# Moving transposes, norm sums, output gates and retention heads in the order of work of a one-core kernel of three blocks

## The reference

```python
# first block: normed and modulated x, projected to heads, joined by gates
o_g = gla_bidir(q, k, v, la_f, la_b, s0_f, s0_b)        # gated linear attention (GLA), 4 heads, values 128 wide
o_n = neighborhood_attention(q, k, v, k_ctx, v_ctx, rpb) # 8 heads of 64, the context as more keys
# each layer: x normed, then
#   MLA attention: keys and values from a normed low-rank part (kv), queries from a normed one (cq)
#   a convolution of 31 taps over the tokens, a norm over 512 channels, SiLU
#   retention: 4 heads of 256, attention weighted by a decay, a norm per head, a gate
# mix = sum over the branches of tanh_gate * (branch @ W), then out projection, norm, FFN, norm
```

## Time and profile before

| | us |
|---|---|
| median of 3 runs | 2898.34 |
| lowest, highest | 2896.63, 2902.26 |
| span of the profiled execution | 2895.1 |
| PE busy in it | 2824.8 |
| first block's attention stage, as PE's records show it | to about 534 |
| layer 0, layer 1 | about 902 to 1898, 1898 to 2893 |

### The profile page before, as it was taken

The page is one execution under the profiler, slowest core; times in us unless marked ns, Lnnn a source line. Parts: engine busy times, 40 slices in busy tenths (PEclk is TensorE's granted clock), DMA queues, the critical chain, the costliest instruction groups (busy, mean ns, idle before and its releaser), DMA issues.

```text
span 2895.1 us, 34427 instructions
## 1 busy us (share of the span) xinstructions
PE 2824.8 (98%) x13718; PEld 2245.6 (78%) x13718; DVE 1293.4 (45%) x1706; ACT 1133.0 (39%) x1687; POOL 1187.0 (41%) x539
## 2 busy tenths in 40 slices
PE   7999999999999999999999999999999999999999
PEld 6787678788888776787788888877767868788887
DVE  5776424511113866835315202277677353341123
ACT  4334643432233555433334222245545233442222
POOL 2123233354443662453444444435624434344442
PEclk9999999999999999999999999999999999999999
DMA  7343223332223211222232222222112212232222
GB/s 256 117 155 129 73 80 103 111 109 98 96 98 126 78 62 37 73 95 73 87 120 84 96 93 102 95 104 79 61 36 73 101 67 102 95 110 95 95 95 80
DMA packets 89278, 277.97 MB, mean 96 GB/s; under 512 B 9952, under 2 KB 10272, under 8 KB 89120
## 3 DMA queue, kind: packets, MB, share of 16 engines
q1 hardware_dynamic: 89120, 275.78, 27.1%
HBM read 268.40 MB, written 7.34 MB: 95 GB/s over the span
## 4 chain that ended last, share of the span: by engine, by line
PE 89%; DVE 8%; ACT 2%; issue 1%; DMA 0%; SPq 0%; DVEq 0%; ACTq 0%
PE bank L1680 23%; PE bank L1682 23%; PE bank L1681 23%; PE bank L1813 2%; PE bank L2006 2%; PE bank L1956 2%; PE bank L1706 1%; PE bank L1731 1%; PE bank L1729 1%; PE bank L1730 1%; PE bank L1698 1%; PE bank L1699 1%; PE bank L1968 1%; PE bank L1997 1%; DVE pageF L2815 1%
## 5 line engine op out<-in xcount | busy, mean ns | idle before, releaser
L2953 POOL TENSOR_TENSOR wlo<-wraw,whi 128x1024 fp32r<-128x1024 f32 x429 | 1040.9, 2429 | 1478.4 <-ACT whi L2035 1462.9
L1680 PE MATMUL bank<-pageR,whi 128*128 128x512 f32 x3184 | 1289.1, 405 | 6.4 <-ACT pageF L2288 1.6
L1682 PE MATMUL bank<-pageR,wlo 128*128 128x512 f32 x3184 | 1231.1, 387 | 0.0
L1681 PE MATMUL bank<-pageR,whi 128*128 128x512 f32 x3184 | 1229.9, 386 | 0.0
L1680 PEld LDWEIGHTS bank<-pageR,whi 128*128 128x128 f32 x3184 | 599.5, 188 | 161.9 <-issue 43.1
L1681 PEld LDWEIGHTS bank<-pageR,whi 128*128 128x128 f32 x3184 | 599.8, 188 | 135.9 <-issue 23.7
L1682 PEld LDWEIGHTS bank<-pageR,wlo 128*128 128x128 f32 x3184 | 598.7, 188 | 123.6
L2035 ACT ACTIVATE whi<-wraw 128x1024 fp32r<-128x1024 f32 x429 | 450.4, 1053 | 409.8 <-PE bank L1682 315.9
L2109 ACT ACTIVATE pageR<-pageF 128x512 fp32r<-128x512 f32 x136 | 85.9, 632 | 436.9 <-DVE pageF L2674 188.5
L2815 DVE SCALAR_TENSOR_TENSOR pageF<-pageF,prm 128x497 f32<-128x497 f32 (+9 forms) x180 | 200.1, 1112 | 2.7
L2669 DVE TENSOR_TENSOR pageF<-bank,pageF 128x512 f32<-128x512 f32 x44 | 30.4, 691 | 211.5 <-PE bank L1682 204.7
(11 more groups left out here) (236 smaller groups left out, 2618.3 us busy)
## 6 DMA issues: line engine op xcount, KB each, us to landing
wraw<-in_wst SPq DMA_DIRECT2D x429, 512.0 KB, 3.4
pageF<-in_wmod SPq DMA_DIRECT2D x96, 256.0 KB, 5.0
pageF<-in_xT SPq DMA_DIRECT2D x16, 256.0 KB, 4.1
pageF<-in_bias SPq DMA_DIRECT2D x16, 256.0 KB, 3.9
kept<-pageF SPq DMA_DIRECT2D x16, 256.0 KB, 4.9
pageF<-kept SPq DMA_DIRECT2D x16, 256.0 KB, 4.0
out_x<-pageF SPq DMA_DIRECT2D x8, 256.0 KB, 2.0
pageF<-in_cT SPq DMA_DIRECT2D x4, 256.0 KB, 10.0
```

The source lines that it names most:

```text
L1680: e.matmul(o, hi, xh, start=first, stop=False)
L1681: e.matmul(o, hi, xl, start=False, stop=False)
L1682: i = e.matmul(o, lo, xh, start=False, stop=last)
L2953: e.tensor_tensor(wlo[:, b % NH, :, :], wraw[:, b % NR, :, :], bc(whi[:, b % NH, :, :]), ALU.subtract).then_inc(*wlod.up(("wlo", b)))
```

## The change

It changes nothing of what is computed, only where steps stand in the plan. (1) Value transposes of GLA stand inside the projection that follows (`turn_gla`), behind its third yield, with heads 0 and 1 in one and 2 and 3 in another; those of the last neighbourhood pair go inside the first `w_ma` projection, and the empty yields beside them are gone. (2) The sums of the `cq`, convolution and retention norms stand one or two rounds later. (3) `side_ret` is a side of its own: it starts when the last pair of attention heads begins to write its values (`("half", l)`), takes its banks from `mb` and waits for pages. (4) `main_branch` runs up to 6 gates ahead, and while pages are short it waits and goes on when 8 are free.

```diff
--- before.py
+++ after.py
@@ -574,7 +574,7 @@
         yield
         for m in range(2):
             if m:
-                yield from proj("wk_g", m, H, HC)
+                yield from turn_gla(0, proj("wk_g", m, H, HC))
             rope_gla(("kg", m), ("o", "wk_g", m))
             if m:
                 evict(("kgc", m), ("oc", "wk_g", m), 256)
@@ -585,10 +585,13 @@
                     yield from proj("wv_g", h, H, HC)
                     evict(("vg_f", h), ("o", "wv_g", h))
                     evict(("vgc_f", h), ("oc", "wv_g", h), 256)
-                if h % 2:
-                    gla_values(h - 1)
+
+    def turn_gla(m, proj_next):
+        for i, _ in enumerate(proj_next):
+            if i == 2:
+                gla_values(2 * m)
+                gla_values(2 * m + 1)
             yield
-            gla_values(2 * m + 1)
 
     def gla_values(h):
         to_tokens(("vg", h), ("vg_f", h), ALL4, mb, ("vg_f", h))
@@ -746,9 +749,6 @@
             yield from proj("wq_na", m, H)
             evict(("raw", "qn", m), ("o", "wq_na", m))
             made.add(("raw", "qn", m))
-        yield
-        yield
-        na_values(3)
 
     def na_values(m):
         to_tokens(("vn", m), ("vn_f", m), ALL4, mb, ("vn_f", m))
@@ -847,7 +847,7 @@
         bias_load(0, 0)
         bias_load(1, 0)
         for h in range(4):
-            yield from proj("w_og", h, H)
+            yield from proj("w_og", h, H) if h else turn_gla(1, proj("w_og", h, H))
             pages.take(("og", h))
             step("silu_gate", h)
             mb.give(("o", "w_og", h), ("og", h))
@@ -883,7 +883,10 @@
     def main_gates1():
         for m in range(8):
             for nm in ("w_ma", "w_mb"):
-                yield from proj(nm, m, H)
+                for i, _ in enumerate(proj(nm, m, H)):
+                    if i == 2 and nm == "w_ma" and m == 0:
+                        na_values(3)
+                    yield
                 pages.take((nm, m))
                 step("tanh_gate", (nm, m), ("o", nm, m))
                 mb.give(("o", nm, m), (nm, m))
@@ -1098,7 +1101,7 @@
             s1.add(("kv", l), 0, ("kv", l))
             for m in range(2):
                 s2.add(("cq", l, m), 0, ("cq", l, m))
-            yield
+            yield from pause(2)
             r = yield from s1.rstd_steps(128, "ones", sbk)
             yield
             step("kv_normed", l)
@@ -1146,6 +1149,8 @@
                 if qt == 0:
                     sbk.take(("mlab", l, j))
                 step("mla_values", l, j, qt)
+                if j == 2 and qt == 0:
+                    made.add(("half", l))
                 for x in (h - 1, h):
                     pages.give(("pt", "mla", (l, x, qt)), ("av", "mla", l, j, qt))
                 if qt == 3:
@@ -1223,8 +1228,7 @@
             sq = Squares(p, ("conv", l))
             for m in range(4):
                 sq.add(("conv", l, m), 0, ("cc", l, m))
-            yield
-            yield
+            yield from pause(4)
             r = yield from sq.rstd_steps(512, "ones", sbk)
             yield
             for m in range(4):
@@ -1270,14 +1274,18 @@
                 pages.give(("tE", l, h, i), ("tD", l, h))
 
         def side_ret():
+            yield from p.ready(("half", l))
+            yield from p.room(8)
             ret_decay(0)
             for h in range(4):
                 yield from p.ready(("rg", l, h, 1))
+                yield from p.room(6)
                 for j in range(4):
-                    sbk.take(("rs", l, h, j))
+                    yield from p.free_banks(mb, 2)
+                    mb.take(("rs", l, h, j))
                     pages.take(("ra", l, h, j))
                     step("ret_scores", l, h, j)
-                    sbk.give(("rs", l, h, j), ("ra", l, h, j))
+                    mb.give(("rs", l, h, j), ("ra", l, h, j))
                     if j % 2:
                         yield
                 pages.give(("rq", l, h), ("rs", l, h, 3))
@@ -1285,18 +1293,18 @@
                 if h < 3:
                     ret_decay(h + 1)
                 for i in range(2):
-                    sbk.take(("ro", l, h, i))
+                    yield from p.free_banks(mb, 2)
+                    mb.take(("ro", l, h, i))
                     step("ret_values", l, h, i)
                     pages.give(("rv", l, h, i), ("ro", l, h, i))
-                    evict(("rof", l, h, i), ("ro", l, h, i), bks=sbk)
+                    evict(("rof", l, h, i), ("ro", l, h, i))
                     yield
                 for j in range(4):
                     pages.give(("ra", l, h, j), ("ro", l, h, 1))
                 sq = Squares(p, ("ret", l, h))
                 for i in range(2):
                     sq.add(("rof", l, h, i), 0, ("rof", l, h, i))
-                yield
-                yield
+                yield from pause(3)
                 r = yield from sq.rstd_steps(256, "ones", sbk)
                 yield
                 yield
@@ -1314,11 +1322,15 @@
             ahead = 0
             gate = lambda m: ("tg", l, 8 * i + m)
             xs = [(key, l, m) for m in range(n)]
-            while (not all(x in made for x in xs) or ahead < 3) and ahead < 4 and len(pages.free) >= 8:
-                yield from proj("w_gate" + L, 8 * i + ahead, X)
-                tanh_scaled(gate(ahead), ("o", "w_gate" + L, 8 * i + ahead))
-                ahead += 1
-            yield from p.ready(*xs)
+            while not all(x in made for x in xs) or ahead < 3:
+                if ahead < 6 and len(pages.free) >= 8:
+                    yield from proj("w_gate" + L, 8 * i + ahead, X)
+                    tanh_scaled(gate(ahead), ("o", "w_gate" + L, 8 * i + ahead))
+                    ahead += 1
+                elif all(x in made for x in xs):
+                    break
+                else:
+                    yield
             for m in range(8):
                 if m >= ahead:
                     yield from p.room(3)
@@ -1341,7 +1353,7 @@
         weave(chain(main_mla(), main_conv(0), main_conv(3), main_ret(0), main_conv(1), main_ret(1), main_conv(2),
                     main_branch(0, "o_mla", 4, "w_mo"), main_branch(1, "o_conv", 4, "w_pw"), main_ret(2), main_ret(3),
                     main_branch(2, "o_ret", 8, "w_ro")),
-              [chain(side_mla(), side_ret()), chain(taps(0), taps(1), taps(2)), taps(3), side_conv_norm()], 1)
+              [side_mla(), side_ret(), chain(taps(0), taps(1), taps(2)), taps(3), side_conv_norm()], 1)
         p.drop(X, ("o", "w_gate" + L, 23))
         pages.give(rs.r, ("tgs", ("tg", l, 23)))
         for name in ("cosr", "sinr"):
```

## The result

The changed kernel takes 2917.86 us (median of 4 runs, 2915.69 to 2919.93), the kernel before 2898.89 beside it: the ratio is 1.0067, with a 95% interval of 1.0053 to 1.0080, 19.0 us slower. I had forecast 2908.8 and a range up to 2917, so the sign was right and the size too small: 10 us were expected, 19 came, just beyond the range. The profiled span is 2916.9 against 2895.1. These 21.8 us are more than the 19.0 of the medians because the profiled execution of the kernel before was one of its quickest. In every run whose own time is listed beside its span, only about 2 us (1.8 to 2.05) lie around the span, not the 3.2 that I had taken.

A forecast was written before the change was run, and what follows sets the result against it. PE, busy 2824.8 of 2895.1 us, was taken as the bound. Two layers at -8.7, +1.6 once for the clock and +5.3 for the first block made 10.5 us slower: span 2905.6, median 2908.8, range 2885 to 2917.

The forecast's parts named there:

- part 5: Six gates ahead: empty rounds behind the convolution's sum leave a new 8.7 us wait before `w_pw`, -10.8 a layer.
- Rival A: Convolution's tail stays covered by at least five rounds of main work, so its loss becomes 0: 2887.2 us; chance 0.22.
- part 1: First block, moved GLA and last neighbourhood value transposes: a gain of 5.3 us (0 to 11).
- Gain 8.0 - 4.9 = 3.1: GLA values 0 and 1: 8.0 us lost before, 4.9 after with a new wait of 3.2 and lower clock.
- +0.5: GLA values 2 and 3 inside the first `w_og` projection: small gain in us (0 to 1.6), still lacking a bank.
- +5.3: Sum of all first-block terms, a gain in us (0 to 11).
- +2.7: First block, transposes at 249.54: their 2.68 us wait falls with the main work two rounds further on.
- part 2: Later norm sums: their waits, 4.8 us a layer, all go; net +4.5 a layer and +1.6 once for the clock.
- 1.4 a layer: Retention head 3: `o_ret` comes a round later, leaving one round less of cover before `w_ro`, a loss in us.
- parts 3 and 4: Retention beside the last attention heads: 8.8 us lost against 6.4 before, -2.4 a layer (+2 to -5).
- The 4.6: New wait in us of the retention head's value products for DVE's decays, standing 3.4 behind their first score.
- Rival C: Dearer: convolution's chain takes 12 us instead of 9, attention's end costs 3.5 a layer: 2917 us; chance 0.12.

The follow-up runs named there:

- cap8b1: The changed kernel with up to 8 gates ahead in branch 1 in place of 6: 2906.76 us, ratio 1.0029.
- gate_all: The kernel before with the new rule for gates ahead, and all 8 gates of branch 1 before its first product: 2892.01 us, ratio 0.9972.
- gate_only: The kernel before with the new rule for gates ahead alone (up to 6, going on when pages are free): 2911.62 us, ratio 1.0048.
- gla_only: The kernel before with the GLA value transposes moved, nothing else: 2902.59 us, ratio 1.0012.
- cq_only: The kernel before with one further round ahead of the kv and cq sums, nothing else: 2906.61 us, ratio 1.0025.
- cqsum: The kernel before with the cq sum alone one round later, the kv norm where it was: 2903.74 us, ratio 1.0017.
- sums_only: The kernel before with the convolution's sum two rounds and the retention heads' sums one round later, nothing else: 2898.98 us, ratio 1.0002.
- half_gate: The kernel before with retention as a side of its own from the half mark and the new rule for gates ahead: 2914.63 us, ratio 1.0051.
- gate_all_conv: The kernel before with the new gate rule, all 8 branch 1 gates before its first product, and the convolution's sum two rounds later: 2895.45 us, ratio 0.9987.

## Why the prediction was right and wrong, point by point

- **The tail of the convolution (part 5)**: right in place, mechanism and size. -10.8 was forecast; the wait of 8.1 and the slots behind it, 1.9 over their usual time, cost 10.0 in either layer. `cap8b1` and `gate_all` show it: cover put back behind the sum takes it away. Net of the sum's wait, the convolution was forecast at -6.8 in layer 0 and -8.4 in layer 1; the balance of the traces gives about -6 and -8. Rival A had its price right (21.6; the 22 between `gate_only` and `gate_all`), but its condition, that gates be left, did not hold.
- **The first block (part 1), the step that failed**: "Gain 8.0 - 4.9 = 3.1" and "+0.5" for values 2 and 3, and with them +5.3 for the block; measured -3.5 in `gla_only` (-6.6 against the quick trace of before). For values 0 and 1 the wait returned at 4.99, with the same lower clock: gain about 0. I had priced the new wait from when ACT had been free before, and didn't ask what bounds the stretch. DVE does (11.43 of 11.70 us in my own row), and by moving products ahead of the transposes nothing of its work goes away. For values 2 and 3 the wait is 5.7, with a granted clock of 0.72 over 12 us. There DVE has idle time, and what failed is that I put next to nothing on ACT's order: two heads together need a bank whose copy stands behind the decays. That is read from the timeline; no run changed this order alone. And the +2.7 for the wait at 249.54 didn't come: 4.3 us of its kind and 3.2 behind DVE (L2549, 1.1 before) stand there now.
- **The cq sum (part 2)**: the second failed step: "All go ... that hangs on the norms comes a round later" named only head 3. `w_uq` reads the cq norm, and the kernel before already had its slack used up, in a row of the waits that I hadn't weighed:

```profile
PE bank L1680 <- ACT pageF L2288: 1.6, 2, 0.8
```

  The eviction of `w_kn` stands on ACT behind the copy of the cq norm. A norm one round later is then paid in full, with DVE steps beside POOL's halves on top (2.76 and 2.57 us for 0.7). Forecast +1.2 a layer, measured about -4 in the changed kernel's trace and 7.3 for both layers in `cq_only`. The `cqsum` run has 4.9 for the cq sum alone; the intervals of the two overlap, so what the kv norm's later place adds is not settled.
- **The other sums (part 2)**: "1.4 a layer" at `w_ro` was right (its sixth slot's loss went from 0.26 to 1.76), and the sums' waits went as said. Alone the later sums bring 0 (`sums_only`), as the waits moved to `w_pw` and `w_ro`. With the tail open they do bring something: in layer 0 `half_gate` waits 2.0 at the convolution's sum and 8.7 behind it, the changed kernel 8.1 in all. This also fits the parts' total, which run alone cost 26 us (3.5, 0, 7.3, 14.8 and 0.6) and together 19, though with intervals of 2.5 to 3.6 us on each that gap is hardly clear of noise.
- **Attention and retention (parts 3 and 4)**: -2.4 forecast, about +2 a layer measured in the changed trace, between the end of the cq norm and the convolution's sum. The 4.6 was mis-read as much as mis-sized: the value products begin 6.3 us behind the first score, not 3.4, as attention work stands between, and don't wait; a score product waits 1.3 for a bank. And the gates run beside the attention, which I had put into those rounds and then counted at nothing, cover the attention's own waits: the earlier trace rows had 5.4 there, after 2.1. `half_gate` against `gate_only` says that the gates do it, not retention.
- **The sum**: the two errors in the layers cancel (cq was forecast 5 a layer too good, the attention 4 too bad). That the layers came out right, 15.8 forecast and 15.5 measured (19.0 less the 3.5 of `gla_only`), was luck. What remains is the first block, 9 us (+5.3 against -3.5), and that is the whole miss within the noise.

Rival C had the time nearly right (2917), by luck too: its chain of 12 us was 10.4, and the attention's end gained.

## What to carry to other kernels

Before moving work to cover a wait, read all engines' busy columns over the stretch: where another engine is at 98%, the wait only changes its name, as it did at values 0 and 1 in four placements here (5.0, 7.1, 3.9 and 6.1 us). Where none is full, read the order of the engine that frees what the moved work needs: at values 2 and 3 the copies stood on ACT behind the decays. For every producer that is made later, look up the reader's wait in the list: a reader that already waits, as `w_uq` did for 0.8 us, has no slack, and paid the whole delay. And work that is pulled forward into gaps is missing where it used to be cover: count what is left behind the next long chain, at the chain's length when its engines are shared (17.3 us to the third tile in `gate_all_conv`, not 11.6), and hold that much back. And one profiled execution is one draw: with the same code, PE came to the same step 5.7 us apart in nine traces, so a difference of a few us between two traces needs the runs beside it.

## What the runs showed of the hardware

DVE steps that read and write pages of SBUF take 0.42 to 0.75 us alone and mostly 2 to 2.9 when they begin beside POOL's work, of which a half of a weight block is 2.4 us long (0.42 became 2.56 at 85.16, 0.69 became 2.57 at 952.07). In the kernel before, 80 of DVE's two-input steps from page to page (128x512, float32) began while POOL was busy, and 56 of them took over 1.5 us; of 358 that began while it was idle, one did. Steps that read a bank were not slowed: 105 of DVE's TENSOR_TENSOR steps from a bank began beside POOL, and all took 0.68 or 0.69. So a round's shift in the plan changes which steps are hit.

After a wait of 8.1 us PE ran at the half clock in both layers (granted 0.50 from 1275.9 to 1279.1, 0.83 over 20 us); in the kernel before, the 2.1 us wait at the same norm brought it in layer 0 and not in layer 1.
